# Expert stage of a two-block transformer kernel: the scatter of the former pair's rows moved between the gate and the up products

## What is computed

```python
# h: 256 tokens x 1024; each token picks 2 of 32 experts, with weights
def expert_block(args):
    tok, wt, e = args
    xb = h_pad[tok]
    y = (jax.nn.silu(xb @ w_gate[e]) * (xb @ w_up[e])) @ w_down[e]
    return y * wt[:, None]
...
out = jnp.zeros((t + 1, d), ys.dtype).at[buf_tok].add(ys.reshape(-1, d))
```

## Time and profile before

| | us |
|---|---|
| median of 3 runs | 1801.99 (1801.14 to 1803.03) |
| profiled execution, own time | 1804.82 |
| its span, first to last instruction | 1803.1 |
| TensorE (PE) busy | 1751.6, 97% of the span |
| VectorE (DVE) busy | 922.0, 51% |
| ScalarE (ACT) busy | 731.4, 41% |
| HBM read | 443.83 MB |

### The profile page before, as it was taken

One profiled execution on the slowest core, in us unless ns is written; L12 is line 12 of the kernel. 1 busy time (PEld: TensorE's weight loads), 2 busy tenths in 40 slices (PEclk: granted clock), 3 DMA queues, 4 the chain that ended last, 5 costly groups with the idle time before them and its releaser, 6 DMA issues.

```text
span 1803.1 us, 26732 instructions
## 1 busy us (share of the span) xinstructions
PE 1751.6 (97%) x11052; PEld 1388.1 (77%) x11052; DVE 922.0 (51%) x1131; ACT 731.4 (41%) x936; POOL 167.9 (9%) x82
## 2 busy tenths in 40 slices
PE   6999999999999989999998999999999999999998
PEld 4887745445453558999997999989999899998886
DVE  4675211111111157666685755676656656566565
ACT  4434211111111145445335544464445655355443
POOL 0200000000000001111001111122111001111110
PEclk9999999999999999999999999999999999999999
DMA  9568999999999976555652455555555655455551
GB/s 365 178 222 316 371 399 428 427 429 428 429 429 427 428 279 207 187 185 155 198 164 71 164 187 187 186 187 190 185 186 198 202 176 177 150 184 179 193 185 60
DMA packets 181072, 446.18 MB, mean 247 GB/s; under 512 B 7958, under 2 KB 139407, under 8 KB 163063
## 3 DMA queue, kind: packets, MB, share of 16 engines
q1 hardware_dynamic: 177504, 437.84, 65.7%
q10 hardware_dynamic: 3062, 4.98, 0.8%
q0 software_dynamic: 416, 2.10, 0.3%
HBM read 443.83 MB, written 1.06 MB: 247 GB/s over the span
## 4 chain that ended last, share of the span: by engine, by line
PE 83%; DMA 8%; DVE 6%; ACT 2%; issue 1%; POOL 0%; SPq 0%; DVEq 0%; ACTq 0%
PE wk L815 16%; PE wk L1286 9%; PE wk L817 8%; PE acc L787 5%; PE acc L788 5%; PE acc L789 5%; PE wk L1313 5%; PE wk L787 3%; DMA arena<-in_w_up_dram 3%; PE wk L788 3%; PE wk L789 3%; PE wk L1242 3%; DMA ex_ring<-in_w_up_dram 2%; PE wk L866 2%; PE wk L867 2%; DVE w_lo L576 2%
## 5 line engine op out<-in xcount | busy, mean ns | idle before, releaser
L576 DVE TENSOR_TENSOR w_lo<-ring,w_hi 128x2048 fp32r<-128x2048 f32 x198 | 452.7, 2289 | 194.4 <-ACT w_hi L567 193.6
L815 PE MATMUL wk<-h_both,w_hi 128*128 128x512 f32 x1344 | 477.1, 399 | 1.4 <-DVE gated L2574 0.8
L567 ACT ACTIVATE w_hi<-ring 128x2048 fp32r<-128x2048 f32 x198 | 377.5, 1907 | 245.7 <-PE acc L789 97.7
L817 PE MATMUL wk<-h_both,w_lo 128*128 128x256 f32 x1344 | 377.3, 281 | 0.0
L815 PEld LDWEIGHTS wk<-h_both,w_hi 128*128 128x128 f32 x1344 | 252.6, 188 | 63.7 <-issue 1.6
L817 PEld LDWEIGHTS wk<-h_both,w_lo 128*128 128x128 f32 x1344 | 253.9, 189 | 0.4
L2132 POOL TENSOR_TENSOR hid_lo<-gated,hid_hi 128x512 fp32r<-128x512 f32 x44 | 124.7, 2834 | 1138.8 <-ACT hid_hi L1939 1138.8
L787 PE MATMUL acc<-hid_hi,w_hi 128*128 128x256 f32 x720 | 204.6, 284 | 1.4 <-DVE arena L2790 0.8
L788 PE MATMUL acc<-hid_lo,w_hi 128*128 128x256 f32 x720 | 203.7, 283 | 0.0
L789 PE MATMUL acc<-hid_hi,w_lo 128*128 128x256 f32 x720 | 203.6, 283 | 0.0
L1947 ACT ACTIVATE gated<-wk 128x512 f32<-128x512 f32 x88 | 52.6, 598 | 241.0 <-PE wk L817 233.2
(11 more groups left out here) (422 smaller groups left out, 2868.1 us busy)
## 6 DMA issues: line engine op xcount, KB each, us to landing
ring<-in_ffn_w_in_dram SPq DMA_DIRECT2D x88, 1024.0 KB, 5.1
ring<-in_ffn_w_out_dram SPq DMA_DIRECT2D x44, 1024.0 KB, 4.9
ring<-in_w_ada_dram SPq DMA_DIRECT2D x24, 1024.0 KB, 6.7
ring<-in_b_w_in_dram SPq DMA_DIRECT2D x24, 1024.0 KB, 5.2
ex_ring<-in_w_gate_dram SPq DMA_DIRECT2D x11, 2048.0 KB, 20.3
ex_ring<-in_w_up_dram SPq DMA_DIRECT2D x10, 2048.0 KB, 22.4
ex_ring<-in_w_down_dram SPq DMA_DIRECT2D x9, 2048.0 KB, 24.7
ring<-in_w_down_dram SPq DMA_DIRECT2D x8, 2048.0 KB, 25.0
```

Source lines behind the costliest of these rows:

```text
L567: nc.scalar.activation(w_hi[:, v % SPLIT, 0:n], ring[:, u % RING, 0:n], ACT.Copy).then_inc(w_hi_ready, 1)
L576: eng.tensor_tensor(w_lo[:, v % SPLIT, 0:n], ring[:, u % RING, 0:n], w_hi[:, v % SPLIT, 0:n].bitcast(F32), ALU.subtract).then_inc(w_lo_rea ...
L815: mm(banks[:, m, :], wh[:, k, f], h_both[:, k, :, :], start=k == 0, stop=False, skip_group_check=True)
L817: last = mm(banks[:, m, T:2 * T], wl[:, k, f], h_hi[:, k, :], start=False, stop=k == KT - 1, skip_group_check=True)
```

## The change

The wait for `y_ready` and the scatter of the former pair stand ahead of step s = 2, between gate and up products. Nothing is added or taken away; the lines behind it move by three (1286 becomes 1289, while 1259, 1297 and 1313 keep their numbers).

```diff
                 for s in range(4):
+                    if s == 2 and p:
+                        pe.wait_ge(y_ready, at(2 * p, 2))
+                        scatter(p - 1)
                     if s % 2 == 0:
                         both_in(s // 2)
...
-                if p:
-                    pe.wait_ge(y_ready, at(2 * p, 2))
-                    scatter(p - 1)
                 pe.wait_ge(ex_hidden, at(p + 1))
```

## The result

The change makes the kernel slower: median of 5 runs 1810.47 us (1809.10 to 1813.94) against 1802.72 (1801.14 to 1804.46) for the kernel before, beside it. The ratio is 1.0045 [1.0033, 1.0057], which is +8.1 us [5.9, 10.3]. The forecast was 1811.4, +9.4.

What follows compares the result with a forecast made beforehand. TensorE's own work was taken to bound the expert stage up to pair 9, the weight stream from pair 10. Added work 18.5, less 8.9 of waits, less 0.2 at the stage's end: +9.4, 1811.4 us; range 1807 to 1815.5.

Steps and rivals of the forecast that it cites:

- insertion between gate and up products: On TensorE in pairs 1 to 15: the scatter there puts the first up matmul 2.24 us later behind the gate products.
- way back to 64 columns: From the last scatter matmul to the first up product: 0.20 us, bounds 0.12 and 0.53, as no row showed it.
- up products to transposes, loop: Without the scatter as cover, transposes follow the last up matmul by 1.45 us, waiting for VectorE's product; before, 2.54.
- a pair of the loop: TensorE's time for each of the loop's 12 pairs: net 1.21 us more, so 28.98 us instead of 27.77.
- all pairs, no cushion: TensorE's added work over 12 loop pairs and pairs 1, 14 and 15: 18.5 us before any waits are deducted.
- cushion: TensorE's waits for up weights in pairs 10 to 15: 8.9 us that added TensorE work can fill for free.
- change of form: Switching TensorE between 64-column products and 128-column scatter matmuls and back: 0.35 us a pair, within the 2.24.
- the FFN's start: TensorE's 3.37 us idle time at the feed-forward layer, put down to ScalarE and taken as unchanged: 0 us.
- The rival in which it hides the scatter: In pairs 10 to 15 the weight stream still bounds TensorE and absorbs the scatter: 1803.3 us, not slower; 7%.
- the one at 260 us: Gap in the weight stream while pair 3's gate weights wait for pair 1's down products: to grow by 1.3 us.
- The rival that it is free: At the scatter's entry and exit, early weight loads make the change of form cost nothing: 1806.1 us; 4%.
- as the rival had it: The clock falls after each pair's new idle time behind the up products: 15 half-clock spells, 37 us more, 1849; 2%.

Runs made afterwards that it cites:

- six_pairs: Scatter moved ahead of the up products only in the loop's six even pairs, against the kernel before: ratio 0.9999, -0.2 us.
- before_light: Kernel before with weight refills of groups 8 to 46 fetching only half of each tile, against the kernel before: ratio 0.9939, -11.0 us.
- by_gather: Scatter placed between the first half of the down products and the gather's second half, against the kernel before: ratio 1.0023, +4.1 us.
- half_early: Eight of 16 scatter matmuls ahead of the up products, eight left behind them, against the kernel before: ratio 0.9998, -0.4 us.
- after_light: Changed kernel with weight refills of groups 8 to 46 fetching only half of each tile, against the kernel before: ratio 1.0050, +9.0 us.
- after_quiet: Changed kernel with SP holding the third FFN weight tile until the last scatter is done, against the kernel before: ratio 1.0036, +6.5 us.
- halves: Kernel before with every expert weight refill cut in two separately released halves, against the kernel before: ratio 1.0020, +3.6 us.
- before_again: Kernel before, rerun without an edit, against the kernel before: ratio 1.0006, +1.1 us.
- after_again: Changed kernel, rerun without an edit, against the kernel before: ratio 1.0054, +9.7 us [7.4, 12.1].

## Why the prediction was right, and where it wasn't

| step | forecast | shown by |
|---|---|---|
| insertion between gate and up products | 2.24 | 2.26, pair 2 of after |
| way back to 64 columns | 0.20 (0.12 to 0.53) | 0.21, the same |
| up products to transposes, loop | 1.45 | 1.45, the same |
| a pair of the loop | 27.77 + 1.21 = 28.98 | 29.00, products of after; 1.23 in six_pairs |
| all pairs, no cushion | 18.5 | 18.8, the light kernels |
| cushion | 8.9 | 8.87 up to the last down matmul, before_light |
| change of form | 0.35 a pair | 0.35 in by_gather, 0.34 in half_early |
| last down matmul | +9.6 | 444.02 for 434.12 behind the product of pair 0: +9.90 |
| end of the stage | -0.2 | 2.94 for 3.30: -0.36 |
| the stage | +9.4 | +9.54 |
| the FFN's start | 0 | -2.3 in the profile of after |

*The cover.* The mechanism is the forecast one: VectorE's product lay under the scatter, and the scatter now lies where nothing needs cover. The whole move costs 18.8 us; half of it is paid with the 8.9 us in which TensorE would have waited for weights. That the net of a single pair is small (1.23 us) and the stage still loses is the count of 15.

*The stream.* The rival in which it hides the scatter wanted 29.3 us a pair and DMA waits left; the pace is 29.00 and there are none. As the prediction had it, its own condition decides: six_pairs puts the total under the cushion, and there the stream does hide it. Where the prediction was off is the place of the hole: it said that the one at 260 us would grow by 1.3. That one stayed at 2.9, and a second one of 1.1 came at 249, from the up products' release, of which the text had said only that it comes 2.2 later. So the later weights are late by about what was forecast, by another wait. With 9.3 us of reserve at pair 15 (forecast 9) neither has an effect on the time.

*The change of form.* The rival that it is free falls: the pace would have been 28.65, as in by_gather, where one such change is in fact spared. The first scatter matmul still follows the last product by 0.53. The Trainium skill's rule of weight loads pulled ahead (TensorE: Matmul & The Clock Gate, Part 2) doesn't help across this change of form, by that row.

*The clock.* No matmul within the stage of after is at half clock: the granted clock is 1.00 in the four windows shown and from 483 to 640 us, through idle times of up to 1.0 us. after_light and after_quiet each have one spell, 3.4 us at 660 us in the last down products, which costs them 1.7 us of their stage, by_gather and halves have one each in the last pair; 15 spells, as the rival had it, are in no execution.

*The step that failed* is "Its idle time comes from ScalarE and stays, so I take 0", on the 3.37 us at the start of the FFN. It took the name that the profile gives to the end of the wait for its cause. `h_both` can't have been it, since TensorE starts 0.66 us behind the start of ScalarE's first `h_both` and 2.60 behind that of the second; what held it was in the DMA queue, and left when the stage grew longer. In the profiles the fifth matmul is 2.0 to 2.3 us sooner, and the rest 2.3 to 3.8 us shorter with the spell of half clock, of the 9.5 that the stage lost. It stayed within the range, and the two measured differences, +8.1 [5.9, 10.3] and +9.7 [7.4, 12.1], lie on both sides of the forecast. That they lie so near it is in part luck, since a term of 2 to 4 us was put at nothing.

*What stays open.* By the stage's 9.5 and the rest's -2.3 to -3.8 the medians should lie 6 to 7 us apart, and they lie 8 to 10. The half-clock spells aren't at the same place in two executions of one kernel (6.8 us from 661.3 in before, from 658.1 in before_again; 3.4 us from 672.2 in after, from 668.4 in after_again), nor is the stage's start, and one profile for each kernel does not tell their mean. That was not settled.

## What to carry to other kernels

Work that covers a wait is worth its cover, not its place: before an independent block is moved ahead of the work that feeds a slower engine, look for the instruction next to it that has no such block (pair 0 here), and its idle time is the price. Then compare the price times the count with the waits that a second resource leaves at the end; what lies under them is free, and what lies over them is paid in full. And when an idle time is put down to an engine that was done long before, look at the DMA queue at that moment, the instruction queues among it.

## What I had not expected of the hardware

- Behind TensorE's branch at the stage's end two instruction packets (8 and 16 KB) share the DMA engines with the weights. TensorE's fifth matmul behind it starts 1.4 to 1.6 us behind the end of the 16 KB packet in 13 of 14 executions; with a weight tile in the queue that is 4.7 us behind `h_both`, without 2.1 to 2.8. Holding one prefetch back for some microseconds made the kernel 4.1 us faster.
- Weight transfers of 1 MB in packets of 8 KB move 421 GB/s with the queue full, those of 2 MB in packets of 16 KB 427 to 428. Which of the two sizes does it was not told apart.
- The way from a 128-column to a 64-column matmul takes 0.20 us where 128 columns stream ahead of it and 0.21 where 256 do.
